# A hybrid attention and recurrence step: cached keys turned in 32x32 blocks on VectorE, scores as 32x32 products

## The reference

```python
# per sequence b: q (8, H, 64), k_past, v_past (4096, H, 64) gathered by page_table (32 pages of 128 keys)
s = einsum('bqhd,bkhd->bhqk', q / 8, k) + c_q - c_k        # forgetting bias, c a running sum of log forget values
p = softmax(concat([s_past, s_new]), -1)
o = p @ v
```

## Time and profile before

| | us |
|---|---|
| median of 3 runs | 1509.98 (1507.31 to 1511.25) |
| the profiled execution | 1510.73 |
| its span in the trace | 1509.0 |
| PE, DVE, ACT busy | 1402.4, 438.2, 357.0 |
| 0 to 329 us: norm, projection, prompt attention | 329 |
| 329 to 925 us: sample attention and recurrence | 596 |
| 925 us to the end: projections and SwiGLU block | 584 |

### The profile page before, as it was taken

The page is one execution under the profiler, slowest core; times in us unless marked ns, Lnnn a source line. Parts: engine busy times, 40 slices in busy tenths (PEclk is TensorE's granted clock), DMA queues, the critical chain, the costliest instruction groups (busy, mean ns, idle before and its releaser), DMA issues.

```text
span 1509.0 us, 27895 instructions
## 1 busy us (share of the span) xinstructions
PE 1402.4 (93%) x11595; PEld 953.3 (63%) x11595; DVE 438.2 (29%) x917; ACT 357.0 (24%) x713; POOL 110.0 (7%) x223
## 2 busy tenths in 40 slices
PE   5999999988799999999989779999999999999997
PEld 4755666655577777777755454477777777744442
DVE  5022355455844444444445241310000000000002
ACT  3010233245444343443433331100000000000011
POOL 6283000000000000001202010000000000000000
PEclk9999899998799999999989889999999999999998
DMA  5187011023898787878957897003111221150001
GB/s 206 57 189 205 7 57 35 1 75 110 284 312 277 229 292 247 294 255 266 272 191 261 315 314 245 1 13 100 56 56 56 89 79 56 56 195 0 0 0 63
DMA packets 123174, 219.32 MB, mean 145 GB/s; under 512 B 11451, under 2 KB 35078, under 8 KB 123046
## 3 DMA queue, kind: packets, MB, share of 16 engines
q1 hardware_dynamic: 115154, 193.64, 38.3%
q0 software_dynamic: 7824, 23.85, 5.9%
q10 hardware_dynamic: 68, 0.02, 0.0%
HBM read 203.06 MB, written 14.41 MB: 144 GB/s over the span
## 4 chain that ended last, share of the span: by engine, by line
PE 84%; DVE 5%; DMA 4%; ACT 3%; issue 2%; SPq 1%; POOL 0%; DVEq 0%; POOLq 0%; ACTq 0%
PE PS L1369 23%; PE PS L736 13%; PE PS L1388 10%; PE PS L1178 6%; PE PS L1192 4%; PE PS L1308 4%; PE PS L1237 4%; PE PS L709 2%; DMA arena<-in_cache_k 2%; DMA out_wkv_prompt<-arena 1%; PE PS L1394 1%; PE PS L992 1%; PE PS L1002 1%; PE PS L996 1%; ACT arena L1622 1%
## 5 line engine op out<-in xcount | busy, mean ns | idle before, releaser
L1369 PE MATMUL PS<-arena 128*128 128x288 f32 x1408 | 342.1, 405 | 1.2 <-DVE arena L2251 1.2
L1369 PEld LDWEIGHTS PS<-arena 128*128 128x128 f32 x1408 | 265.7, 189 | 77.4 <-DVE arena L2251 1.4
L736 PE MATMUL PS<-arena 128*128 128x301 f32 (+1 forms) x736 | 197.7, 426 | 0.0
L1622 ACT ACTIVATE arena<-PS 128x512 f32<-128x512 f32 x256 | 141.4, 596 | 192.8 <-PE PS L1178 192.4
L1178 PE MATMUL PS<-arena 128*128 128x128 f32 x1024 | 153.8, 296 | 27.1 <-DMA arena<-in_cache_k 15.1
L736 PEld LDWEIGHTS PS<-arena 128*128 128x128 f32 (+1 forms) x736 | 136.6, 189 | 54.7 <-issue 13.6
L1178 PEld LDWEIGHTS PS<-arena 128*128 128x128 f32 x1024 | 122.1, 151 | 55.8 <-issue 24.2
L1388 PE MATMUL PS<-arena 128*128 128x512 f32 x352 | 151.5, 592 | 1.5 <-DVE arena L2277 1.5
L1388 PEld LDWEIGHTS PS<-arena 128*128 128x128 f32 x352 | 66.5, 189 | 86.2 <-issue 84.3
L2277 DVE TENSOR_TENSOR arena<-PS,arena 128x576 f32<-128x576 f32 x22 | 16.7, 758 | 327.0 <-ACT arena L1686 327.0
L1686 ACT ACTIVATE arena<-PS 128x576 f32<-128x576 f32 x22 | 14.3, 651 | 329.8 <-PE PS L1369 329.8
(11 more groups left out here) (360 smaller groups left out, 1409.9 us busy)
## 6 DMA issues: line engine op xcount, KB each, us to landing
arena<-in_cache_k SPq DMA_DIRECT2D x256, 256.0 KB, 4.3
arena<-in_cache_v SPq DMA_DIRECT2D x256, 256.0 KB, 4.8
arena<-in_w_gate SPq DMA_DIRECT2D x11, 1024.0 KB
arena<-in_w_up SPq DMA_DIRECT2D x11, 1024.0 KB
arena<-in_w_in SPq DMA_DIRECT2D x5, 2048.0 KB, 11.9
forgets_after<-arena POOLq DMA_DIRECT2D x64, 128.0 KB, 8.5
arena<-forgets_after SPq DMA_DIRECT2D x32, 256.0 KB, 5.1
arena<-in_w_down SPq DMA_DIRECT2D x4, 2048.0 KB
```

The lines of the kernel that those rows point to most:

```text
L736: ins = mm(PS[0:width, bank, 0:HALF], wring[:, c % 2, k, c0:c0 + width], xnT[:, k, half * HALF:(half + 1) * HALF], start=(k == 0), stop=(k ...
L1369: ins = mm(PS[:, 4 * (f % 2) + 2 * w + half, 0:HO], fring[r % FR][:, c:c + P], hT[:, k, half * HO:(half + 1) * HO], start=(k == 0), stop=( ...
L1622: av(KTs[:, (2 * i + q) % LOT], PS[:, T_USE[("k", L, i, q)] % 2, :].rearrange("p (g n) -> p g n", g=NG), ACT.Copy)\
```

## The change

Key pages stay where DMA put them. DVE transposes two pages at a time in place, in blocks of 32x32 (`turn_keys`, now 128x1024, two a half lot, 128 in all). In a page so turned, the partitions 32a to 32a+31 hold 32 of a head's 64 values for the keys 32a to 32a+31. A score is then the sum of two products with 32 rows each, and the queries are laid out anew for that (`QX` for all sequences, filled in the prompt attention by 16 DVE copies; `QS`, in the place of `sel`, filled by ACT for each pair). `page_scores` has two parts a half lot, each of 64 matmuls with a 32x32 stationary and 32x64 moving operand, on two of the four row groups, which write two PSUM banks; a part starts when the one before it has ended. The bias is added in two halves, one a bank. The key ring now has three slots of half a lot (four pages each). The turned probabilities are copied by ACT instead of DVE, L1241 is gone, PSUM bank 0 alone takes all transposes. The order of steps in a lot is new on PE, ACT and DVE, with eight steps as before. The page loads are written out without a loop, in the order: key half, values, bias, key half. The low-rank weights go to another place and wait for the prompt's logarithms. The new-state products of two heads are issued side by side, and start when both masked operands are there. The diff, cut to its core:

```diff
-        QB = new(DB, NG, 32)
+        QX = new(DB, H, 2, DS)
...
-        SCORE, OUT = 2, 3
+        TURN, SCORE, OUT = 0, [2, 1], 3
...
-        KTs = at(qT_off + 2 * NG * RAW + FOXW, LOT, NG, P)
+        QS = sel.rearrange("p h n -> p (h n)").rearrange("p (q h d n) -> p q h d n", q=2, h=H, d=2)
+        KN = kTS.rearrange("p g n -> p (g n)")
...
-        Kr = at(X0 + 2 * LOTC, LOT, 2, FOXW)
+        KH = [at(off, 2, 2, FOXW) for off in (X0 + 2 * LOTC, X0 + 2 * LOTC + 2048, qT_off + 2 * NG * RAW + FOXW)]
...
+            sp.wait_ge(S["log_ready"], 1)
...
+            def load_bias(L):
+                if L >= 2:
+                    sp.wait_ge(S["sc_taken"], 2 * (L - 1))
+                pr, j = L // NLOT, L % NLOT
+                sp.dma_start(Rr[:, L % 2, :], biases[pr * P:(pr + 1) * P, LOTC * j:LOTC * (j + 1)]).then_inc(S[f"r_in{L % 2}"], 16)
+
+            def key_half(L, hh, numbers):
+                n = 2 * L + hh
+                sp.wait_ge(S["k_free"], 3 + max(n - 2, 0))
+                for i in range(2):
+                    for q in range(2):
+                        sp.dma_start(KH[n % 3][:, i, q, :], k_pages[bass.ds(numbers[q][2 * hh + i], 1)].rearrange("o p n -> p (o n)"))\
+                            .then_inc(k_in[n % 3], 16)
+
+            def value_page(L, i, numbers):
+                sp.wait_ge(S["v_free"], LOT * L + i + 1)
                 for q in range(2):
-                    sp.dma_start(ring[:, i, q, :], pages[bass.ds(numbers[q][i], 1)].rearrange("o p n -> p (o n)"))\
-                        .then_inc(landed[i], 16)
-
...
+            of_lot = lot_numbers(0)
+            sp.wait_ge(S["k_free"], 3)
+            for hh in range(2):
+                key_half(0, hh, of_lot)
+            load_bias(0)
+            after = lot_numbers(1)
+            key_half(1, 0, after)
+            for L in range(LOTS):
+                if L and L + 1 < LOTS:
+                    key_half(L + 1, 1, after)
+                for i in range(LOT):
+                    value_page(L, i, of_lot)
+                if L + 1 < LOTS:
+                    load_bias(L + 1)
+                    if not L:
+                        key_half(L + 1, 1, after)
+                    of_lot = after
+                if L + 2 < LOTS:
+                    after = lot_numbers(L + 2)
+                    key_half(L + 2, 0, after)
 
             sp.wait_ge(S["rwkv_done"], 1)
...
-                    for hp in range(2):
-                        h = 2 * g + hp
-                        hc = slice(h * HD, (h + 1) * HD)
-                        pe.wait_ge(S["um_ready"], h + 1)
-                        o = PS[64 * hp:64 * hp + 64, E + 2 + g % 2, :]
-                        if g >= 2 and hp == 0:
-                            pe.wait_ge(S["sn_taken"], g - 1)
-                        mm(o, nat_[64:P, K_, hc], Um[64:P, h % 2, 1].rearrange("p b i -> p (b i)"), start=True, stop=False)
-                        ins = mm(o, nat_[64:P, B_, hc], Um[64:P, h % 2, 0].rearrange("p b i -> p (b i)"), start=False, stop=True)
-                        ins.then_inc(S["sn_ready"], 1)
+                    pe.wait_ge(S["um_ready"], 2 * g + 2)
+                    if g >= 2:
+                        pe.wait_ge(S["sn_taken"], g - 1)
+                    for w, u in ((K_, 1), (B_, 0)):
+                        for hp in range(2):
+                            hc = slice((2 * g + hp) * HD, (2 * g + hp + 1) * HD)
+                            ins = mm(PS[64 * hp:64 * hp + 64, E + 2 + g % 2, :], nat_[64:P, w, hc],
+                                     Um[64:P, hp, u].rearrange("p b i -> p (b i)"), start=(u == 1), stop=(u == 0), skip_group_check=True)
+                            if u == 0:
+                                ins.then_inc(S["sn_ready"], 1)
...
-            def turn_keys(L, i):
-                pe.wait_ge(k_in[i], 32 * (L + 1))
-                for q in range(2):
-                    bank = t_bank(("k", L, i, q))
-                    for g in range(NG):
-                        ins = tr(PS[:, bank, g * P:(g + 1) * P], Kr[:, i, q, g * P:(g + 1) * P], ident)
-                    ins.then_inc(S["k_free"], 1)
-
-            def page_scores(L, i):
-                if i == 0:
-                    if L % NLOT == 0:
-                        pe.wait_ge(S["nmn_ready"], L // NLOT + 1)
-                    if L:
-                        pe.wait_ge(S["sc_taken"], L)
-                pe.wait_ge(S["kt_taken"], 2 * LOT * L + 2 * i + 2)
-                for gg in range(2):
-                    for q in range(2):
-                        for gp in range(2):
-                            g = 2 * gp + gg
-                            ins = mm(PS[ROWS[2 * q + gp], SCORE, i * P:(i + 1) * P], QB[:, 2 * (L // NLOT) + q, g, :],
-                                     KTs[:, (2 * i + q) % LOT, g, :], start=(gg == 0), stop=(gg == 1), skip_group_check=True)
-                ins.then_inc(S["sc_page"], 1)
+                return TURN
+
+            def page_scores(L, hh, part):
+                n = 2 * L + hh
+                if part == 0:
+                    if hh == 0:
+                        if L % NLOT == 0:
+                            pe.wait_ge(S["nmn_ready"], L // NLOT + 1)
+                        if L:
+                            pe.wait_ge(S["sc_taken"], 2 * L)
+                    pe.wait_ge(S["kt_ready"], 2 * n + 2)
+                else:
+                    pe.wait_ge(S["sc_part"], n + 1)
+                a0 = 2 * (part ^ hh)
+                for hm in range(4):
+                    for d in range(2):
+                        for a in (a0, a0 + 1):
+                            for q in range(2):
+                                for gp in range(2):
+                                    h = 4 * gp + hm
+                                    o = PS[ROWS[2 * q + gp], SCORE[a % 2], 2 * P * hh:2 * P * hh + 2 * P].rearrange("p (i n) -> p i n", i=2)
+                                    ins = mm(o[:, :, 32 * a:32 * a + 32], QS[ROWS[a], q, h, d],
+                                             KH[n % 3][ROWS[a], :, q, 64 * h + 32 * d:64 * h + 32 * d + 32],
+                                             start=(hm + d == 0), stop=(hm + d == 4), skip_group_check=True)
+                ins.then_inc(S["k_free"] if part else S["sc_part"], 1)
 
...
-                if half:
-                    mm(PS[:, OUT, 511:512], ident, ones[:, 0:1], start=False, stop=True, skip_group_check=True).then_inc(S["ov_ready"], 1)
...
-                    turn_keys(L, 0)
-                    yield
-                    turn_keys(L, 1)
-                    page_scores(L, 0)
-                    yield
+                    page_scores(L, 0, 0)
                     if L:
                         turn_probs(L - 1)
                     yield
-                    turn_keys(L, 2)
-                    page_scores(L, 1)
+                    page_scores(L, 0, 1)
                     yield
                     if L:
                         lot_values(L - 1, 0)
                     if j == 0:
                         turn_new(pr)
                     yield
-                    turn_keys(L, 3)
-                    page_scores(L, 2)
-                    yield
                     if L:
                         lot_values(L - 1, 1)
                     yield
-                    page_scores(L, 3)
+                    page_scores(L, 1, 0)
+                    yield
+                    if j == 0 and L:
+                        turn_output(pr - 1)
+                    page_scores(L, 1, 1)
+                    yield
                     if j == 0:
-                        if L:
-                            turn_output(pr - 1)
                         new_values(pr)
+                    yield
                     if j == NLOT - 1 and pr + 1 < NPAIR:
                         new_scores(pr + 1)
                     yield
...
-            def take_keys(L, i):
-                for q in range(2):
-                    act.wait_ge(S["k_free"], 2 * LOT * (L + 1) + 2 * i + q + 1)
-                    if L or i >= 2:
-                        act.wait_ge(S["sc_page"], LOT * L + i - 1)
-                    av(KTs[:, (2 * i + q) % LOT], PS[:, T_USE[("k", L, i, q)] % 2, :].rearrange("p (g n) -> p g n", g=NG), ACT.Copy)\
-                        .then_inc(S["kt_taken"], 1)
+            def take_probs(L):
+                act.wait_ge(S["pr_turned"], L + 1)
+                av(PTs, PS[:, TURN, :].rearrange("p (a n) -> p a n", a=LOT), ACT.Copy).then_inc(S["pr_taken"], 1)
+
+            def fill_queries(pr):
+                if pr:
+                    act.wait_ge(S["k_free"], 3 + 2 * pr * NLOT)
+                else:
+                    act.wait_ge(S["qx_ready"], 1)
+                to = QS.rearrange("p q (b m) d n -> p (q b) m d n", m=4)
+                of = QX[:, 2 * pr:2 * pr + 2].rearrange("p q (b m) d t -> p (q b) m d t", m=4)
+                for m in range(4):
+                    ins = av(to[:, :, m, :, 8 * m:8 * m + 8], of[:, :, m], ACT.Copy)
```

(46 more changed lines are left out.)

148 lines of the change are left out of this document (49 added, 99 removed).

## The result

The changed kernel takes 1810.94 us (median of 4 runs, 1810.23 to 1821.29) against 1510.62 (1507.31 to 1512.75): ratio 1.2006, 95% interval 1.1958 to 1.2055. The prediction said 1492 and a range of 1440 to 1560, so it has the wrong sign. Span after: 1809.7 us, mean granted clock 0.826 (before 0.969).

A forecast was written before the change was run, and what follows sets the result against it. PE was taken to bound the middle of the sample attention. Middle -25, tail -5, head +8, new scores +2 and prompt attention +2 gave -18 us: 1492 from a median of 1509.98, range 1440 to 1560.

The forecast's parts named there:

- Its fetches lie beside the page loads; nothing, or part of the second rival.: PE's instruction stream about doubles; its fetches were to cost nothing, or part of the second rival.
- the second rival: Issue decides: score passes go no faster than 14.6 ns, a part takes 2.07 us; +62 us, 1572; chance 0.13.
- about 325 us at the same clock: Middle of the sample attention (400 to 750 us before): its 20.75 lots shorten to about 325 us, clock unchanged.
- 7.3 ns a pass: Score passes on eight 32x32 tiles in turn: 7.3 ns each, so 1.14 us a part and 4.6 us a lot.
- The third rival: Score passes at 24.5 ns: 13.3 us a lot, 190 us more and 20 for the rest, 1720; chance 0.04.
- DVE: DVE's 128 block transposes of 128x1024 in the sample attention: 1.2 us each, 4.8 us a lot.
- the stall: PE idle before a lot's first score part, waiting for DVE's transpose: 0.9 us a lot, some 20 us in all.
- The head: Start of the sample attention: DVE waits for four pages and turns them, first score later than 340 us; 8 us more.
- State products at nothing: New-state products of two heads side by side: no difference (0 to 3 us more, and nothing less).
- New scores: New scores of the first and three later pairs: 4 x 128 passes at 7.3 ns against 0.43 us a block, 2 us more.
- L1241: The one-column matmul, once a lot, goes: 0.31 us of PE a lot saved.

The follow-up runs named there:

- e4: The changed kernel with the scores of one head in four only, 4096 passes in place of 16384: 1525.93 us, ratio 1.0094 to the kernel before.
- e2: The changed kernel with only the first half of each head's features in the scores, 8192 passes of 64 columns: 1617.05 us, ratio 1.0695 to the kernel before.
- e8: The kernel before with four more DVE reductions of 128x1024 a lot, whose results no one waits for: 1563.73 us, ratio 1.0352.
- e1: The kernel before with only the new-state products of two heads issued side by side: 1513.52 us, ratio 1.0015.
- e7: The kernel before without the one-column matmul L1241, DVE waiting for the values' signal instead: 1506.1 us, ratio 0.9973.
- e3: The changed kernel with each score pass made for one page of two, 16384 passes of 32 columns: 1798.06 us, ratio 1.1892 to the kernel before.
- e6: The changed kernel with four useless full-array matmuls of 64 columns ahead of each score part: 1912.72 us, ratio 1.2662 to the kernel before.

## Why the prediction was wrong

- **"Its fetches lie beside the page loads; nothing, or part of the second rival."** This is one of two steps that failed, and stands behind most of the 149 us of idle time. I asked only whether the fetches compete for DMA, not whether they come in time. The forecast used up a block of 256 instructions in the 1.14 us of a part; PE went on no sooner than 2.16 us after the start of the packet that it waited for. It ran dry in 68 pauses, 172 us; 129.0 us of the idle time that "issue" ended are at L1179.
- **The clock was left at 1.00** ("about 325 us at the same clock"). This is the other step, and as large: it was no term of the sum. The clock fell to 0.67, and the other work of PE became some 138 us longer (150.3 - 11.8). Why it fell is open. I had read the row of the head at 0.78 and of the tail at 0.90 and not asked what the change would do to it.
- **7.3 ns a pass** was mis-sized even in clean parts at full clock: 1.48 us a part, less 0.21 for the last pass, over 127 is 10.0 ns (the part that carried a forecast of 1.14 us). At the low clock a part took some 2 us (123 passes in 1.98, the chain row below). All in all a pass cost 22 to 24 ns. Drawn back to no passes from e4 and e2, the kernel would take 1526 - 91 = 1435 us (an estimate): 75 below the kernel before, and 16384 passes put 376 on it, against 128 x 1.14 = 146 in the forecast. The third rival, at 24.5 ns, had nearly this price. It gave 1720 since it set the full 6.7 us a lot, 214 us, against it; 75 is what was left of them.
- **DVE** was right in its size, 1.2 us forecast and 1231 ns measured, and so was the stall: "some 20 us in all", 22.3 measured (L2097). But it was small because PE was slow: with a quarter of the passes it is 36.8 us, and e8 puts 53 us on the load. A forecast of faster passes should have had the larger stall.
- **The head**: "first score later than 340 us" was wrong. DVE's first two transposes took 2.37 us from 332.87 and the first score part started at 335.92 (the timeline below).
- **State products at nothing** was right (e1). **New scores** at 2 us more: four blocks of 128 passes took 6.0 us against 4 x 0.43, 4.3 more. **L1241** at 0.31 us a lot, 9.9 us, brought 4.6 (e7).
- **The second rival** named the mechanism nearest to it, "issue decides", but bounded it by the longest stream in the trace, 14.6 ns. Those streams were 32 passes long and used up a quarter of a block of instructions, so they could not show what a block costs.

Timeline of the head, the new scores' group and a row of the chain of waits, kernel after:

```profile
332.87 2.37 DVE L2097 STREAM_TRANSPOSE arena<-arena 128x1024 f32<-128x1024 f32 x2 [6.37 <-DMA arena<-in_cache_k]
...
335.92 3.87 PE L1179 MATMUL PS<-arena 32*32 32x64 f32 x232 [4.53 <-DVE arena L2128]
...
L1196 PE MATMUL PS<-arena 32*32 32x32 f32 x512 | 6.0, 228 | 3.0 <-ACT arena L1648 3.0
```

```profile
611.69 1.98 PE PS L1179 x123
```

## What to carry to other kernels

Before work is cut into small tiles, count the instructions, and look where they stand. Over the whole stretch the supply seems ample: 170 blocks at the shortest distance of 3.3 us are 561 us of 882.6. It fails locally, where a block of 256 is used up in 1.5 us. Don't leave the clock out of the sum either: the loss on work that the change did not touch (138 us) was nearly the whole price of the transposes that it took away (153.8). An experiment that keeps the sum of columns and doubles the passes (e3 against e2) tells the two apart in one pair of runs.

## What was not expected of the hardware

PE stood still 68 times, for 172 us, on one place modulo 256 in its instructions, and went on 1.19 to 1.58 us after the end of a packet of its instruction queue; in 35 of them the packet started only after PE had stopped. The granted clock of the middle was 0.67 in e6 with PE busy 297.5 of 350 us and 0.97 in e8 with 301.9. Putting 864 transposes in front of the score parts of e4 raised it from 0.80 to 0.91 and made the kernel 8 us longer for 122 us of work. A transpose in 32x32 blocks of 128x1024 fp32 on DVE took 1231 ns, 1.2 ns an element of a partition.
